# Expert loop of a two-layer model kernel: the seven extra blocks in turns 1 to 7 in place of 0 to 6

## What is computed

```python
def grouped_moe(h, w_router, router_bias, w_gate, w_up, w_down):
    t = h.reshape(-1, D)                       # 256 tokens x 1024
    scores = jax.nn.sigmoid((t @ w_router).astype(jnp.float32))
    ...
    combine = (jax.nn.one_hot(eidx, N_EXPERTS, dtype=jnp.float32) * w[..., None]).sum(-2)   # 2 of 16 experts
    y = jnp.zeros(t.shape, jnp.float32)
    for e in range(N_EXPERTS):
        he = jax.nn.silu(t @ w_gate[e]) * (t @ w_up[e])
        y = y + combine[:, e:e + 1] * (he @ w_down[e]).astype(jnp.float32)
```

## Time and profile before

| what | us |
|---|---|
| median of 3 runs | 2116.42 (2114.01 to 2120.44) |
| the profiled execution | 2111.29 |
| its span | 2109.5 |
| PE busy in it | 1879.9 (89%) |
| first pass of the expert loop, first gate_up to end of last down | 404.9 to 685.3 |
| second pass | 1047.0 to 1310.3 |

### The profile page before, as it was taken

The page is one execution under the profiler, slowest core; times in us unless marked ns, Lnnn a source line. Parts: engine busy times, 40 slices in busy tenths (PEclk is TensorE's granted clock), DMA queues, the critical chain, the costliest instruction groups (busy, mean ns, idle before and its releaser), DMA issues.

```text
span 2109.5 us, 26017 instructions
## 1 busy us (share of the span) xinstructions
PE 1879.9 (89%) x10453; PEld 1306.3 (62%) x10456; DVE 582.5 (28%) x1087; ACT 533.9 (25%) x923; POOL 80.7 (4%) x137
## 2 busy tenths in 40 slices
PE   4799998588999499999499998499979999987998
PEld 1467767333333368868333333377779997677998
DVE  1134142100000225142200000332255552235554
ACT  1000331111111210231111111205045442444543
POOL 0000000011110000000011111000000000000000
PEclk9899999699999699999699999699989999998999
DMA  9975543699999446453699999266955453222450
GB/s 393 426 315 239 202 160 149 259 427 406 418 416 407 182 177 245 192 204 116 253 428 420 416 421 404 114 275 277 364 219 197 182 196 134 106 120 103 176 199 20
DMA packets 54478, 546.30 MB, mean 259 GB/s; under 512 B 7280, under 2 KB 11632, under 8 KB 23408
## 3 DMA queue, kind: packets, MB, share of 16 engines
q1 hardware_dynamic: 42656, 505.66, 59.5%
q0 software_dynamic: 11728, 39.33, 4.7%
HBM read 590.58 MB, written 27.79 MB: 293 GB/s over the span
## 4 chain that ended last, share of the span: by engine, by line
PE 82%; DMA 9%; DVE 4%; issue 2%; DVEq 1%; ACT 1%; POOL 1%; SPq 0%; POOLq 0%; ACTq 0%; PEldq 0%
PE bank L830 25%; PE bank L1107 13%; PE bank L1131 7%; PE bank L795 6%; PE bank L796 6%; PE bank L797 6%; PE bank L840 4%; DMA ring<-in_w_up 4%; DMA ring<-in_ada 3%; PE bank L1241 2%; PE bank L944 1%; PE bank L901 1%; PE bank L1310 1%; PE bank L1224 1%; PE bank L1081 1%
## 5 line engine op out<-in xcount | busy, mean ns | idle before, releaser
L830 PE MATMUL bank<-h_t,ring 128*128 128x256 f32 (+1 forms) x1824 | 408.0, 385 | 24.0 <-DVE h_t L1924 20.7
L830 PEld LDWEIGHTS bank<-h_t,ring 128*128 128x128 f32 (+1 forms) x1824 | 347.4, 192 | 80.6 <-issue 19.6
L795 PE MATMUL bank<-split_x,split_w 128*128 128x256 f32 x1024 | 288.7, 282 | 1.1 <-DVE split_w L2192 1.1
L796 PE MATMUL bank<-split_x,split_w 128*128 128x256 f32 x1024 | 288.2, 281 | 0.0
L797 PE MATMUL bank<-split_x,split_w 128*128 128x256 f32 x1024 | 288.2, 281 | 0.0
L1107 PE MATMUL bank<-ring,h_t 128*64 128x512 f32 x1024 | 231.5, 603 | 11.8 <-DMA ring<-in_w_up 9.0
L795 PEld LDWEIGHTS bank<-split_x,split_w 128*128 128x128 f32 x1024 | 194.5, 190 | 2.9 <-DVE split_w L2192 2.9
L796 PEld LDWEIGHTS bank<-split_x,split_w 128*128 128x128 f32 x1024 | 194.5, 190 | 0.0
L797 PEld LDWEIGHTS bank<-split_x,split_w 128*128 128x128 f32 x1024 | 194.4, 190 | 0.0
L2192 DVE TENSOR_TENSOR split_w<-ring,split_w 128x1024 fp32r<-128x1024 f32 x128 | 156.3, 1225 | 91.2 <-ACT split_w L1636 91.2
L1107 PEld LDWEIGHTS bank<-ring,h_t 128*64 128x64 f32 x1024 | 83.7, 139 | 144.5 <-issue 142.4
(11 more groups left out here) (306 smaller groups left out, 1794.8 us busy)
## 6 DMA issues: line engine op xcount, KB each, us to landing
ring<-in_ada SPq DMA_DIRECT2D x48, 2048.0 KB, 11.7
ring<-in_w_gate SPq DMA_DIRECT2D x32, 2048.0 KB, 12.9
ring<-in_w_up SPq DMA_DIRECT2D x32, 2048.0 KB, 18.3
ring<-in_w_down SPq DMA_DIRECT2D x32, 2048.0 KB, 15.1
ring<-in_mlp_w SPq DMA_DIRECT2D x32, 2048.0 KB, 8.6
ring<-in_w_in SPq DMA_DIRECT2D x16, 2048.0 KB, 8.6
mix<-in_w_gate SPq DMA_DIRECT2D x14, 2048.0 KB
mix<-in_w_up SPq DMA_DIRECT2D x14, 2048.0 KB
```

The costliest lines, as they stand in the source:

```text
L795: pe.matmul(out, hi, x_hi, start=start, stop=False, **kw)
L796: pe.matmul(out, hi, x_lo, start=False, stop=False, **kw)
L830: ins = pe.matmul(bank[0:width, place * T:place * T + T], w_ap[:, k, c0:c0 + width], rhs[:, k, :], start=(k == 0), stop=(k == nk - 1))
```

## The change

A constant FIRST_X = TURNS - XB = 1 is added, and extra block q stands in turn q + 1: turn 0 has two blocks and turns 1 to 7 have three. `xx` is in turns 1, 3, 5, 7. Everything that was indexed by i for the extra blocks (expert number, flag, rows in DRAM, semaphore counts) is indexed by i - FIRST_X. A turn without an extra block now runs xp of the next turn between hidden_rows e1 and down e1; before, the only such turn was the last and had no xp. The number of instructions is the same on every engine. The core of the diff:

```diff
@@ moe constants @@
-BLOCKS = [(i, b) for i in range(TURNS) for b in range(3) if b < 2 or i < XB]
+FIRST_X = TURNS - XB
+BLOCKS = [(i, b) for i in range(TURNS) for b in range(3) if b < 2 or i >= FIRST_X]
...
-RAW = [(i, b) for i in range(TURNS) for b in (0, 2) if b == 0 or (i % 2 == 0 and i < XB)]
+RAW = [(i, b) for i in range(TURNS) for b in (0, 2)
+       if b == 0 or (i >= FIRST_X and (i - FIRST_X) % 2 == 0)]
...
@@ SP queue @@
                     if (i, 2) in NUMBER:
-                        if i == 0:
+                        if i == FIRST_X:
                             sp.wait_ge(DV.sem, DV.at("rows of tokens", l))
                             sp.wait_ge(scattered, l * 64 + 64)
-                        e = sp.value_load(extra[0:1, i:i + 1], min_val=0, max_val=NE - 1)
-                        used = sp.value_load(extra[0:1, XB + i:XB + i + 1], min_val=0, max_val=1)
+                        q = i - FIRST_X
+                        e = sp.value_load(extra[0:1, q:q + 1], min_val=0, max_val=NE - 1)
+                        used = sp.value_load(extra[0:1, XB + q:XB + q + 1], min_val=0, max_val=1)
                         for j, name in enumerate(matrices):
-                            if i:
+                            if q:
                                 n = NUMBER[i - 1, 2]
...
@@ PE, a turn @@
-                    if x is not None:
-                        if i % 2 == 0:
-                            token_rows(i, 2)
-                        down(e0)
-                        gate_up(x, range(0, 6))
-                        hidden_rows(e1)
+                    if (i, 2) in RAW:
+                        token_rows(i, 2)
+                    down(e0)
+                    if x is not None:
+                        gate_up(x, range(0, 6))
+                    hidden_rows(e1)
+                    if x is not None:
                         gate_up(x, range(6, KT))
                         down(e1)
                         hidden_rows(x)
-                        token_rows(i + 1, 0)
-                        down(x)
-                    else:
-                        down(e0)
-                        hidden_rows(e1)
-                        down(e1)
+                    if i + 1 < TURNS:
+                        token_rows(i + 1, 0)
+                    down(e1 if x is None else x)
...
@@ POOL queue @@
-                    if i:
+                    if (i - 1, 2) in NUMBER:
                         store(NUMBER[i - 1, 2])
-                    if (i, 2) in RAW:
+                    if (i, 2) in RAW and i + 1 < TURNS:
                         pool.wait_ge(MP.sem, MP.at(f"xx{i}", l))
                         block_rows(i + 1, 0)
                     store(NUMBER[i, 0])
                     store(NUMBER[i, 1])
+                store(NUMBER[TURNS - 1, 2])
```

More of the change, by code:

```diff
@@ L332, in moe_steps @@
         e0, e1, x = NUMBER[i, 0], NUMBER[i, 1], NUMBER.get((i, 2))
-        pe += [f"gu{e0}", f"hT{e0}", f"gu{e1}"]
-        act += [f"sg{e0}", f"hT{e0}", f"sg{e1}"]
+        xx, xp = [f"xx{i}"] * ((i, 2) in RAW), [f"xp{i + 1}"] * (i + 1 < TURNS)
+        pe += [f"gu{e0}", f"hT{e0}", f"gu{e1}"] + xx + [f"d{e0}", f"hT{e1}"]
+        act += [f"sg{e0}", f"hT{e0}", f"sg{e1}"] + xx + [f"out{e0}", f"hT{e1}"]
         dve += [f"h{e0}", f"h{e1}"]
         if x is not None:
-            pe += [f"xx{i}"] * (1 - i % 2) + [f"d{e0}", f"hT{e1}", f"gu{x}", f"d{e1}", f"hT{x}", f"xp{i + 1}", f"d{x}"]
-            act += [f"xx{i}"] * (1 - i % 2) + [f"out{e0}", f"hT{e1}", f"sg{x}", f"out{e1}", f"hT{x}", f"xp{i + 1}",
-                    f"out{x}"]
+            pe += [f"gu{x}", f"d{e1}", f"hT{x}"] + xp + [f"d{x}"]
+            act += [f"sg{x}", f"out{e1}", f"hT{x}"] + xp + [f"out{x}"]
             dve += [f"h{x}"]
         else:
-            pe += [f"d{e0}", f"hT{e1}", f"d{e1}"]
-            act += [f"out{e0}", f"hT{e1}", f"out{e1}"]
+            pe += xp + [f"d{e1}"]
+            act += xp + [f"out{e1}"]
     return pe + four("yT"), act + ["y0", "y1"], dve + ["y0", "y1"]
@@ L1088, in weights_full @@
                     if b == 2:
-                        pe.wait_ge(extra_full[j], l * (16 * XB) + 16 * (i + 1))
+                        pe.wait_ge(extra_full[j], l * (16 * XB) + 16 * (i - FIRST_X + 1))
                     else:
@@ L1096, in gate_up @@
                     if part[0] == 0:
-                        pe.wait_ge(MA.sem, MA.at(f"xx{i - i % 2}" if b == 2 else f"xp{i}", l))
+                        pe.wait_ge(MA.sem, MA.at(f"xx{i - (i - FIRST_X) % 2}" if b == 2 else f"xp{i}", l))
                         if n > 1:
@@ L1102, in gate_up @@
                     gu = expert_weights(b)[:, 0:2 * SLOT].rearrange("p (u k c) -> p u k c", u=2, k=KT)
-                    half = i % 2 if b == 2 else b
+                    half = (i - FIRST_X) % 2 if b == 2 else b
                     xT = (xxT if b == 2 else xpT)[:, :, CAP * half:CAP * half + CAP]
@@ L1354, in block_rows @@
                 def block_rows(i, b):
-                    at = CAP * (NE + i) if b else P * i
+                    at = CAP * (NE + i - FIRST_X) if b else P * i
                     pool.dma_start(raw, x_rows[at:at + P, :]).then_inc(raw_full, 16)
@@ L1361, in store @@
                     i, b = BLOCKS[n]
-                    at = CAP * (NE + i if b == 2 else 2 * i + b)
+                    at = CAP * (NE + i - FIRST_X if b == 2 else 2 * i + b)
                     for g in range(2):
@@ L1545, in _ @@
                         gated(x)
-                    expert_out(e1)
-                    if x is not None:
+                        expert_out(e1)
                         hidden_rows(x)
+                    if i + 1 < TURNS:
                         token_rows(i + 1, 0)
-                        expert_out(x)
+                    expert_out(e1 if x is None else x)
                 for t in range(TT):
```

## The result

The changed kernel takes 2156.3 us (median of 4 runs, 2153.2 to 2159.3) for 2115.2 of the kernel before (4 runs): a ratio of 1.0196, 95% interval 1.0181 to 1.0211, so it is 41 us slower. The forecast was 2149, slower, with a range of 2131 to 2166.

A forecast was written before the change was run, and what follows sets the result against it. PE and DMA were taken to run level in the expert loop, extra blocks giving loads time to keep up. Loop passes +25.5 and +22.5, ends -15, sum +33 on the 2116.4 median: 2149 us, range 2131 to 2166.

The forecast's parts named there:

- What bounds the kernel: Expert loop: PE and DMA run level, 33.4 or 34.6 us a full turn; used extra blocks bring 6.3 MB each.
- The clock of the loader: Loop loads: bytes at 427 GB/s, 1.5 us to start, 3.7 to land; fitted to the landing at 449.28.
- Just through: Second-pass sum: turn 1's first two loads just finish when its first down is issued at 424.6; queue full from 426.1.
- Both causes: Loop: extra 0's load behind turn 1's six loses about 14 us of DMA; short turn 0 wants weights about 12 sooner.
- The loop's sum: Both passes of the expert loop: +22.5 us in the first and +25.5 in the second.
- The ends: PE's idle time behind both passes: 16.4 us for 23.8 and 25.2, taken as -15 us; bounds 0 and -22.6.
- The bound's store: Behind each pass: last store at 3.8 us, idle 13.2 in all, giving the ends' bound of -22.6 us.
- The rest costs nothing: Outside loop and ends: same instruction counts, 20 us of cover for turn 1's row read, xp fills a wait; no cost.
- The loop never catches up: Rival, turns 3 to 7: each late by up to 1 us, some +8, 2157 us; chance 0.12.
- DMA has more to give: Rival, loop loads: DMA could reach 520 GB/s with more queued, 2109 us; chance 0.03, and 0.04 for about no change.
- The ends gain nothing: Rival, behind both passes: the gather is slow by nature, 2164 us; chance 0.08.
- Their full bound: Rival, behind both passes: the ends gain their full bound, -22.6 us, 2141 us; chance 0.13.

The follow-up runs named there:

- e1: Not a run: the second of the two experts of a turn of the expert loop; it has no measured time of its own.
- e0: Not a run: the first of the two experts of a turn of the expert loop; it has no measured time of its own.
- the other eleven: The eleven follow-up experiments, variants of the kernel before or the changed one in load place, load order, extra weights, short turn or held loads; 2091.2 to 2151.1 us.
- the hold: Next stage's loads of slots 2 to 5 issued only when the gathers have landed: 2099.6 us on the kernel before, 2148.2 on the changed one.

## Why the prediction was right, point by point

- **What bounds the kernel**: right. PE and DMA run level in the loop, and the used extra blocks tip it. Without their weights not one wait for DMA is left in the loop of before (the experiment without extra weights).
- **The clock of the loader**: right. Turn 2's second expert was to land at 495.5 and landed at 496.0, turn 3's was put at 543.8 and landed at 543.2. The constants taken from one stretch of before (427 GB/s, 1.5 us to start, 3.7 to land) carried over to another order of loads for turn 2. The 1.5 is no row of its own but what the other terms left of that stretch, so its agreement with 449.28 was no test; turn 2's landing was. Turn 3's adds 48.3 us read off before, and it took 47.1. "Just through" at turn 1 was wrong by little: the queue ran thin for a few us, 1.4 us of transfer, which the error of the constants hid, and that was luck.
- **Both causes**: right, and each shown by a run. The place of extra 0's load is 26 of the 41 us; the short turn in front costs about as much in the loop (14.3 and 11.6), and the ends' gain of 11 leaves 13.5 to 15 of it. The first wait was put at 8 to 10 us and is 11.3 and 11.1; extra 0's at 2 to 4, and it didn't wait, turn 2's e0 waited 0.8 in its place. The sum was unmoved, as said.
- **The loop's sum**: +48 forecast, +52.0 measured. First pass +24.7 for 22.5, second +27.3 for 25.5. Two terms were too small. The 24 matmul records behind the last wait took 2.7 and 2.4 us more than the 5.37 of a pass without waits, where I had taken 1.4 (in the first pass as an amount that stands before and after alike and so drops out). And the last turn took 34.8 us (676.70 to 711.46) for 33.6: ACT's wait of 0.87 stands before its last down as before, because this turn has no xp to cover it; I had put it on turn 0 alone.
- **The ends**: -15 forecast, -11.3 measured; no single term was further off. The idle time came down to 18.3 and 19.4, not to the 16 to 17 given as a sign. The gathers came nearly as put (6.6 for 5.9, saving 5.3 in the first pass). The store was mis-sized: 7 us, and it takes 8.2 in the first pass, hardly less than the 8.4 of before, and 9.2 in the second, for 10.5 before. Slot 5's load is issued 5.8 us ahead of the store; DMA still moves 351 GB/s from 711.5 to 720.7, and with that load held the store takes 5.5 and 5.1. I had reckoned when the queue would be empty, but not that a store issued before that would take nearly as long as before. The bound's store of 3.8 us had no row behind it; alone it took 3.3 and 4.3.
- **The rest costs nothing**: right within what a single profile tells; the remainder of the changed kernel, 1523.6, lies inside the 1521 to 1526 of the other eleven, and only the 1516.8 of before lies outside.
- **The rivals.** "The loop never catches up": no; turns 4 to 7 don't wait. "DMA has more to give": no; 428 GB/s with several loads queued, as before. "The ends gain nothing": no, they gain 11.3. "Their full bound", 22.6 us: the ends can give just that (13.3 and 14.3 us with the hold, 21.4 less than before), but not by this change, which leaves the store where it was.

The net error is 8 us: 33 forecast, 41 measured, 4 of it in the loop and 3.7 in the ends. Both parts erred the same way, so nothing cancelled between them.

## What to carry to other kernels

Where loads and TensorE run level over a loop, lay out the bytes that must pass before each matmul, in the order of issue: a load that moves while the queue would stand empty is all but free (the second pass of before took 263.3 us with extra 0's load and 262.6 without any), and the same load behind six others cost 26 us here in two passes. A short turn belongs where nothing follows that is loaded during it. Waits for DMA in one stretch are mostly pieces of one sum, so judge a change by its last wait. And look at what is prefetched for the next stage while a store and a gather stand on the critical path: holding these loads back for 20 us took 21 us from the two ends here, of which 14.5 were left in the time.

## What the hardware showed

- A store of two DMAs of 128 KB from the POOL queue took 3.3 and 4.3 us alone (first and second pass), 5.5 and 5.1 with the tail of three 2 MB loads of the SP queue before it, and 8.2 and 9.2 with a fourth queued; in the kernel before, where the four loads are issued 0.9 to 5.9 us ahead of it, 8.4 and 10.5. Four gathers of 0.5 MB, issued 1.3 us apart, had their first two landed 6.5 us after the first issue when alone, and the other two by 10.1 us (700.75); in company the first two took 11.9 and 11.2. I had expected 3.8 and 5.9.
- The granted clock behind a wait (0.89 and 0.90 over the two stretches of the changed kernel from 449.0 to 544.6, 1.00 in a turn without waits): after waits of 9.1 to 11.6 us the same 24 matmul records took 6.8 to 8.3 us for 5.37, and not in the order of the waits (11.22 gave 7.17, 9.89 gave 8.10 in one execution). So such a wait costs 1.4 to 2.9 us more than its length, where it is the last.
- A full DMA queue is as regular as this: bytes over 427 GB/s, plus 1.5 us to start and 3.7 to land, was fitted to one landing of before (449.28) and told one of the changed kernel, 70 us after the queue filled, to within 0.5 us; nine loads on, a step read off before (48.3 us) told the next to within 0.6.
